# Layer A's dilated attention: the first group in time order with two key chunks, its softmax joined to the others' by shares

## What is computed

```python
DILATED_PAIRS = ((128, 1), (512, 4), (2048, 16))     # window, dilation of each group
def mixer_a(hn, w_in, w_out, q_gain, k_gain, t5_bias):
    proj = hn @ w_in                                  # 3 groups x (q, k, v), and a gate
    ...
    for g, (window, dilation) in enumerate(DILATED_PAIRS):
        q = rms_norm(qkv[:, :, g, 0], q_gain[g])
        k = rms_norm(qkv[:, :, g, 1], k_gain[g])
        v = qkv[:, :, g, 2]
        reach = (window // 2) // dilation             # keys at 0, +-d, ..., +-reach*d
        o, lse = dilated_group_attention(q, k, v, t5_bias[...], dilation, reach)
        outs.append(o)
        lses.append(lse)
    alpha = jax.nn.softmax(jnp.stack(lses), axis=0)   # groups merged by their denominators
    y = jnp.sum(alpha[..., None] * jnp.stack(outs), axis=0)
    y = y.reshape(b, s, BRANCH_WIDTH).astype(hn.dtype) * jax.nn.silu(gate)
    return y @ w_out
```

## Time and profile before

| | value |
|---|---|
| median of three runs | 1672.38 us |
| the profiled execution: its own time | 1674.71 us |
| its span (first to last instruction) | 1672.9 us |
| mean granted TensorE clock | 0.978 |
| busy share PE, DVE, ACT, POOL | 94%, 45%, 46%, 47% |
| layer A in it | about 26 to 712 us |
| mean of one low part on POOL (L919, 128x512; L899, 128x1024) | 1293 ns; 2477 ns |

### The profile page before, as it was taken

The page is one execution under the profiler, slowest core; times in us unless marked ns, Lnnn a source line. Parts: engine busy times, 40 slices in busy tenths (PEclk is TensorE's granted clock), DMA queues, the critical chain, the costliest instruction groups (busy, mean ns, idle before and its releaser), DMA issues. The chain is left out here.

```text
span 1672.9 us, 29914 instructions
## 1 busy us (share of the span) xinstructions
...
## 2 busy tenths in 40 slices
...
GB/s 180 120 59 94 71 96 80 76 101 67 101 70 104 74 90 1 63 149 139 143 154 134 76 51 88 115 70 63 26 28 3 4 3 28 88 89 101 90 92 57
DMA packets 247185, 135.44 MB, mean 81 GB/s; under 512 B 24390, under 2 KB 241518, under 8 KB 246999
## 3 DMA queue, kind: packets, MB, share of 16 engines
...
...
## 5 line engine op out<-in xcount | busy, mean ns | idle before, releaser
L919 POOL TENSOR_TENSOR a_sq_low<-a_sq,a_sq_high 128x512 fp32r<-128x512 f32 x48 | 62.1, 1293 | 278.4 <-ACT a_sq_high L766 278.4
L318 PE MATMUL a_proj<-h_low,w_high 128*128 128x512 f32 x472 | 190.0, 402 | 1.6 <-POOL h_low L938 0.8
L899 POOL TENSOR_TENSOR w_low<-a_w_raw,w_high 128x1024 fp32r<-128x1024 f32 x64 | 158.5, 2477 | 65.8 <-ACT w_high L733 65.8
L320 PE MATMUL a_proj<-h_high,w_high 128*128 128x512 f32 x472 | 185.7, 393 | 0.0
L319 PE MATMUL a_proj<-h_high,w_low 128*128 128x512 f32 x472 | 184.8, 392 | 0.0
L899 POOL TENSOR_TENSOR w_low<-b_w_raw,w_high 128x1024 fp32r<-128x1024 f32 x40 | 100.4, 2512 | 97.1 <-ACT w_high L733 97.1
L318 PE MATMUL b_proj<-h_low,w_high 128*128 128x512 f32 x288 | 116.5, 405 | 1.4 <-POOL h_low L938 0.8
L320 PE MATMUL b_proj<-h_high,w_high 128*128 128x512 f32 x288 | 113.5, 394 | 0.0
L319 PE MATMUL b_proj<-h_high,w_low 128*128 128x512 f32 x288 | 113.2, 393 | 0.0
L819 ACT ACTIVATE a_pt<-a_turned 128x512 f32<-128x512 f32 x64 | 37.8, 591 | 155.8 <-PE a_turned L612 155.8
L318 PEld LDWEIGHTS a_proj<-h_low,w_high 128*128 128x128 f32 x472 | 88.8, 188 | 23.4 <-DVE a_qk L969 3.2
...
## 6 DMA issues: line engine op xcount, KB each, us to landing
a_w_raw<-in_a_w_in_dram SPq DMA_DIRECT2D x78, 512.0 KB, 3.7
b_w_raw<-in_b_w_in_dram SPq DMA_DIRECT2D x30, 512.0 KB, 4.1
b_ada_w<-in_ada_w_dram ACTq DMA_DIRECT2D x24, 512.0 KB, 3.7
f_wt<-in_w_in_dram SPq DMA_DIRECT2D x19, 512.0 KB, 3.8
...
sparse_w_raw<-in_w_in_dram SPq DMA_DIRECT2D x17, 512.0 KB, 3.8
a_w_raw<-in_a_w_out_dram SPq DMA_DIRECT2D x8, 512.0 KB, 3.6
b_w_raw<-in_b_w_out_dram SPq DMA_DIRECT2D x8, 512.0 KB, 3.6
```

Source lines behind the costliest of these rows:

```text
L318: nc.tensor.matmul(out, lh, rl, start=first, stop=False)
L320: return nc.tensor.matmul(out, lh, rh, start=False, stop=last)
L899: nc.gpsimd.tensor_tensor(low(slot_of(b)), raw[:, n % RAW, :, :], high(slot_of(b)), ALU.subtract).then_inc(s_wl, 1)
L919: nc.gpsimd.tensor_tensor(sql[:, :], sq[:, u % 2, :], sqh[:, :], ALU.subtract).then_inc(s_sql, 1)
```

## The change

`attention_layer(nc, T, I, a)` is replaced by a function of its own, `dilated_attention` (layer B keeps `attention_layer`). Group 0's queries are now grouped in order of time: tile t holds 128 consecutive tokens, and its keys are 256 consecutive tokens, in two chunks of 128. Groups 1 and 2 stay by residue. So a step has 4 key chunks a head instead of 6. Since a token of group 0 and the same token of groups 1 and 2 lie in different tiles and rows, each part has its own peak and total; when all four tiles have them, they are copied crosswise between partitions (`swap`), and a chain on DVE and ACT (`shares`, `weights`) makes each part's share, with which the probabilities are then scaled. v of group 0 is projected as an eighth ring unit (V0, features by tokens) and turned at the end of the period (VT); the v units are 256 wide. The output of a pair is gathered in a bank of its own over the four tiles. The gate's reciprocal on DVE is two instructions on ACT. The bias of a head comes in 17 DMAs from the SP queue, 34 for a pair, ahead of the next weight block. In the last pair (`LAST`) three output units begin early (`e` for units 0 and 1, `f` for unit 2).

```diff
+    NQK, GATE, V0, VT = 6, 6, 7, 12
+    UNITS, NR, VB, RAW = 13, 8, 2, 2
+    EARLY, ROWS = 3, 4
+    STEPS = PAIRS * ROWS
+    VW = 3 * P
+    WIN, BIAS = 256, 6 * P
+    V_AFTER = (2, 4)
+    ROLL = ((16, 0, 112), (0, 112, 128))
+    HEAD_BANKS = [0, 1, 2, 3, 4, 5, 6, 0, 1, 2, 3, 1, 0]
+    IN_SCORES, IN_TURNED, IN_O = 11, 6, 7
+    SQUARES_AT = [(2, 5), (3, 3), (4, 2), (5, 1), (6, 1), (6, 6)]
...
+    PERIOD = [("S", 0), ("u", 0), ("S", 1), ("u", 1), ("S", 2), ("u", 2), ("S", 3), ("u", 3), ("u", 4),
+              ("T", 0), ("u", 5), ("A", 0), ("T", 1), ("u", 6), ("A", 1), ("T", 2), ("u", 7), ("A", 2), ("T", 3), ("u", 8),
+              ("u", 9), ("A", 3), ("u", 10), ("u", 11), ("u", 12)]
+    LAST = [("S", 0), ("e", 0), ("S", 1), ("e", 1), ("S", 2), ("e", 2), ("S", 3), ("e", 3), ("e", 4), ("e", 5),
+            ("e", 6), ("T", 0), ("f", 0), ("f", 1), ("A", 0), ("T", 1), ("f", 2), ("f", 3), ("A", 1), ("T", 2), ("f", 4), ("f", 5),
+            ("A", 2), ("T", 3), ("f", 6), ("A", 3), ("e", 7), ("f", 7)]
+    plan = lambda p: PERIOD if p < PAIRS - 1 else LAST
...
+            def load_bias(head):
+                h = head % 2
+                if head >= 2:
+                    sp.wait_ge(s_l2, 8 * (head // 2 - 1) + 7 + h)
+                at = lambda row, x: head * A_ROWS * REL + row * REL + x
+                for n, (x0, j0, j1) in enumerate(((80, 16, 32), (112, 0, 32), (80, 0, 32), (112, 0, 16))):
+                    for c in range(4):
+                        dst = bias[32 * c:32 * c + 32, h, n * P:(n + 1) * P].rearrange("p (c j) -> p c j", c=4)[:, :, j0:j1]
+                        sp.dma_start(dst, bass.AP(tensor=I["scr_a"].tensor, offset=at(c, x0 + j0),
+                                                  ap=[[1, 32], [REL, 4], [1, j1 - j0]])).then_inc(s_bias[h], 16)
+                sp.dma_start(bias[:, h, 4 * P:], bass.AP(tensor=I["scr_a"].tensor, offset=at(7, 0),
+                                                         ap=[[1, P], [REL, 2], [1, P]])).then_inc(s_bias[h], 16)
...
+            sp.wait_ge(T.s_scr, 128)
+            sp.wait_ge(s_neg, 4)
+            for head in range(2):
+                load_bias(head)
+            bias_after = {place["ring", NR * p + 6 + RING]: p for p in range(1, PAIRS)}
+            for n in range(RAW, len(order)):
+                sp.wait_ge(s_wl, n - RAW + 1)
+                load(n)
+                if n in bias_after:
+                    for h in range(2):
+                        load_bias(2 * bias_after[n] + h)
...
+                elif u == VT:
+                    pe.wait_ge(s_pf, UNITS * p + V0 + 1)
+                    for c in range(4):
+                        mm = nc.tensor.transpose(out[:, c * P:(c + 1) * P], vfm[:, c * P:(c + 1) * P], T.ident)
+                else:
+                    c = u - NR
+                    if c == 0:
+                        pe.wait_ge(s_wl, place["v", p, VB - 1] + 1)
...
+            def scores(p, t):
+                if t == 0:
+                    pe.wait_ge(s_pf, UNITS * p + NQK if p else IN_SCORES)
+                if p or t:
+                    pe.wait_ge(s_l2, 2 * (4 * p + t))
+                for n in range(4):
+                    for h in range(2):
+                        hp = slice(h * HD, (h + 1) * HD)
+                        g, k0 = (0, 32 * ((t + n) % 4)) if n < 2 else (n - 1, t * P)
+                        keys = qk[hp, p % 2, 2 * g + 1, :]
+                        keys = runs(keys, k0, k0 + 32) if g == 0 else keys[:, k0:k0 + P]
+                        out = ps_s[:, h, n * P:(n + 1) * P]
+                        mm = nc.tensor.matmul(out.rearrange("p (c j) -> p c j", c=4) if g == 0 else out,
+                                              qk[hp, p % 2, 2 * g, t * P:(t + 1) * P], keys, start=True, stop=True)
+                        if n == 3:
+                            mm.then_inc(s_S, 1)
...
+            def apply_v(p, t):
+                if t == 0:
+                    pe.wait_ge(s_pf, UNITS * (p + 1) if p else UNITS)
+                    if p:
+                        pe.wait_ge(s_y, p)
+                pe.wait_ge(s_pa, 4 * p + t + 1)
+                pe.wait_ge(s_pbk, 4 * p + t + 1)
+                for c, (tile, g) in enumerate(((t, 0), ((t + 1) % 4, 0), (t, 1), (t, 2))):
+                    for h in range(2):
+                        o = ps_o[h * HD:(h + 1) * HD, :]
+                        into = by_time(o)[:, :, 3 - t, :] if g == 0 else o[:, (3 - t) * P:(4 - t) * P]
+                        moving = pt[:, h, c, :].rearrange("p (c j) -> p c j", c=4) if g == 0 else pt[:, h, c, :]
+                        mm = nc.tensor.matmul(into, vt[:, p % 2, tile, g * P + h * HD:g * P + (h + 1) * HD], moving,
+                                              start=(t == 0 and c == 0), stop=(t == 3 and c == 3), skip_group_check=True)
+                mm.then_inc(s_O, 1)
...
+            def exps(p, t):
+                for h in range(2):
+                    act.wait_ge(s_l2, 2 * (4 * p + t) + h + 1)
+                    for part in range(2):
+                        e = probs[:, t, h, part * WIN:(part + 1) * WIN]
+                        nc.scalar.activation(e, e, ACT.Exp, scale=-1.0, bias=stat[:, own, part, t, h, 0:1],
+                                             accum_out=stat[:, own, part, t, h, 1:2]).then_inc(s_exp, 1)
+            def weights(p):
+                act.wait_ge(s_chain, CHAIN * p + 3)
+                nc.scalar.activation(diff[:, :, :], diff[:, :, :], ACT.Exp).then_inc(s_ew, 1)
...
+            def soft_peak(p, t):
+                n = 4 * p + t
+                if p:
+                    dve.wait_ge(s_Ta, n - 3)
+                    dve.wait_ge(s_Tb, n - 3)
+                for h in range(2):
+                    dve.wait_ge(s_bias[h], 16 * 17 * (p + 1))
+                    dve.wait_ge(s_S, 2 * n + h + 1)
+                    tiles = bias[:, h, 0:4 * P].rearrange("p (n j) -> p n j", n=4)
+                    near = tiles[:, 0:2, :] if t == 0 else tiles[:, 2:4, :] if t == 3 else tiles[:, 2:0:-1, :]
+                    two = lambda a: a.rearrange("p (n j) -> p n j", n=2)
+                    nc.vector.tensor_tensor_reduce(two(probs[:, t, h, 0:WIN]), two(ps_s[:, h, 0:WIN]), near, -1.0, HUGE,
+                                                   ALU.add, ALU.min, stat[:, own, 0, t, h, 0:1])
+                    nc.vector.tensor_tensor_reduce(probs[:, t, h, WIN:], ps_s[:, h, WIN:], bias[:, h, 4 * P:], -1.0, HUGE,
+                                                   ALU.add, ALU.min, stat[:, own, 1, t, h, 0:1]).then_inc(s_l2, 1)
+            def swap(p, t):
+                dve.wait_ge(s_exp, 4 * (4 * p + t + 1))
+                for b in range(4):
+                    rows, into = slice(32 * b, 32 * b + 32), slice(32 * (3 - t), 32 * (3 - t) + 32)
+                    nc.vector.tensor_copy(stat[into, other, 1, 3 - b, :, :], stat[rows, own, 0, t, :, :]).then_inc(s_swap, 1)
+                    nc.vector.tensor_copy(stat[into, other, 0, 3 - b, :, :], stat[rows, own, 1, t, :, :]).then_inc(s_swap, 1)
+            def shares(p):
+                done = lambda i: dve.wait_ge(s_chain, CHAIN * p + i)
+                flat = lambda who, s: stat[:, who, :, :, :, s].rearrange("p q t h -> p (q t h)")
+                dve.wait_ge(s_swap, 32 * (p + 1))
+                nc.vector.tensor_tensor(lead[:, :], flat(own, 0), flat(other, 0), ALU.min).then_inc(s_chain, 1)
+                done(1)
+                for who in (own, other):
+                    nc.vector.tensor_tensor(diff[:, who, :], lead[:, :], flat(who, 0), ALU.subtract).then_inc(s_chain, 1)
+                dve.wait_ge(s_ew, p + 1)
+                nc.vector.tensor_tensor(lead[:, :], diff[:, other, :], flat(other, 1), ALU.mult).then_inc(s_chain, 1)
+                nc.vector.tensor_tensor(flat(other, 0), diff[:, own, :], flat(own, 1), ALU.mult).then_inc(s_chain, 1)
+                done(5)
+                nc.vector.tensor_tensor(lead[:, :], lead[:, :], flat(other, 0), ALU.add).then_inc(s_chain, 1)
+                done(6)
+                nc.vector.reciprocal(lead[:, :], lead[:, :]).then_inc(s_chain, 1)
+                done(7)
+                nc.vector.tensor_tensor(share[:, :, :, :].rearrange("p q t h -> p (q t h)"), diff[:, own, :], lead[:, :],
+                                        ALU.mult).then_inc(s_chain, 1)
+                done(8)
+            def normal(p, t):
+                for h in range(2):
+                    for part in range(2):
+                        e = probs[:, t, h, part * WIN:(part + 1) * WIN]
+                        nc.vector.tensor_scalar(e, e, share[:, part, t, h:h + 1], None, ALU.mult).then_inc(s_pn, 1)
...
+            for u in range(UNITS):
+                take(0, u)
+            for p in range(PAIRS):
+                for kind, i in plan(p):
+                    if kind == "S":
+                        soft_peak(p, i)
+                        swap(p, i)
+                        if i == 3:
+                            shares(p)
```

(15 more changed lines are left out.)

418 lines of the change are left out of this document (388 added, 30 removed).

## The result

The changed kernel takes 1737.39 us (median of 4 runs, 1735.57 to 1738.91) against 1672.20 for the kernel before: a ratio of 1.0388, 95% interval 1.0370 to 1.0406. It is slower by 65 us, outside the range of the prediction. Its profiled execution took 1738.8, its span is 1737.0.

The account below looks back on a forecast made before the run. PE's own work was taken to bound the seven full periods. Start +3.7, periods -9.7 and last pair -12.0 gave -18.0: from 1674.7 to 1656.7, or 1654 us since the profiled run lay 2.3 over the median; range 1640 to 1708.

Parts of the forecast that it names:

- PE's work: In a full period of layer A, PE's own work without waits falls by 4.7 us to 72.2.
- The first wait: In each period PE waits 1.9 us (0.5 to 3.5) for unit 4's bank, behind the joined softmax on DVE.
- The second wait: 34 bias DMAs on SP's weight queue delay a load ACT needs; PE waits 0.2 us before the last application of v.
- q: Time SP needs to start one bias piece: taken as 0.50 us, bounds 0.37 to 0.64.
- Rival A: Bias pieces starve the weights: at 0.64 us each, PE waits 5.0 us per period; 1709 us in all, chance 0.34.
- The clock behind both waits: Loss at half clock after PE's waits in a full period: 0.85 us charged, half of an earlier 1.6.
- The start: Start of layer A: PE waits 7.7 us behind the 34 pieces; first scores come 3.7 us later (0 to 9).
- The last pair: From its first scores to the last product's end: 64.4 us, 12.0 less (8 to 14).

Follow-up runs that it names:

- the four edits: Changed kernel with y's rounding ahead of the exponentials, bias DMAs one weight block later, unit 2's take ahead of the shares, reductions for copies: 1653.1 us.
- five edits: The four edits plus the first two heads' 34 bias pieces issued after the load of the ninth block: 1643.9 us, ratio 0.9826.
- all six edits: The kernel with five edits, but in the last pair ACT rounds two blocks of y ahead of each tile: 1639.4 us, ratio 0.9804.

## Why the prediction was wrong

**PE's work: right.** I had 72.2 us for a period without waits; with the four edits it is 72.76, and with five PE is busy for 72.66 of 73 at clock 1.00. The product of 256 columns, which I had to read off a line at 0.121, is 0.117 (304.47 to 305.64 are ten of them). The Trainium skill (TensorE: Matmul & The Clock Gate, Back-to-back issue gap), which gives the formula that I used for an isolated product, has 0.109; the measurement decides. A block of scores costs 1.09 from its start to the next (123.86 to 124.95 in the kernel after), 1.07 forecast. In the period behind 240.21 of the kernel with five edits the four v units take 11.4 for 12.0, the four steps 11.8 for 11.4, the eight units with their sums 48.7 for 47.9, and 0.3 is a wait for a unit's squares. The gain that the change was to bring is there in the main: 3.7 us a period on the mean of seven, 4.1 against the 76.88 of one full step, where I had 4.7.

**The first wait: the step that failed is "Eight small copies at the pace of the small ones (three in 0.28) take 0.7".** The frame was right: exponentials start 3.1 us after unit 2 (3.2 forecast), end at 5.1 (5.2), PE wants unit 4 at 7.3 (7.2), the take costs 0.75 (0.75). But the copies take 3.1 (129.12 to 132.25) and not 0.7, and 2.1 of the 2.4 missing are one copy held by POOL. The shares cost 1.8 for 1.5 and the scalings 1.1 for 0.8. So the wait was 4.66 and not 1.9, outside my own 0.5 to 3.5, which varied only how long an operation works. POOL's low parts of 2.48 stood in my own sum for the second wait, and I never laid one beside DVE's copies. (My terms add up to 8.95 and not to 9.1; that slip is small.)

**The second wait: q was right, the landing was not.** I took 0.50 for a piece; 32 of 34 cost 0.478. The step that failed is "then the next weight load, 3.7 to land": with the median of all loads the block is there 28.6 us after unit 4 ended. It was there at 31.0: the pieces began at 7.8 (7.9 forecast) and took 17.8 for 17.0, with the last at 1.89, and the load behind them landed after 5.4 and not 3.7. PE arrives after 30.2 (30.0 forecast), so a sum that left 1.4 us of slack before the two operations on ACT met a chain that was 2.4 longer, and PE waits 2.33 on the mean for 0.2. Rival A named this mechanism and the right place, but tied it to q of 0.64 and began it at 0.55; it came at 0.478. Of its price for the clock, 2.2 us a period, 1.4 came (the experiment with the bias DMAs later). That A's period of 82.2 is nearly the measured 82.12 is luck: A had 1.9 and 5.0 us for the two waits, and they are 4.66 and 2.33.

**The clock behind both waits.** I charged 0.85 us, half of what the earlier trace rows showed behind a wait of 2.08, as if two waits cost no more than one. Of the period of 82.12, 72.75 are work and 7.0 waits; what is left, 2.4, is the half clock behind them, nearly three times my figure.

**The start: right.** +3.7 forecast, +3.8 measured, with 8.6 us of waiting for 7.7. Part of that is luck, since here too the load behind the 34 pieces (16.3 us, 17 forecast) was there after 5.5 us and not 3.7, while from unit 4's first product to the first scores it took 39.1 us for 40.1.

**The last pair: the step that failed is "192 output products 44.5", taken as work that fills the waits for the tiles.** I gave 3 us to the tiles and let the output products fill the rest, without asking who makes their input. Each needs y's high part from ACT and the low part from POOL, and ACT has it in the program behind the exponentials of the same tile, whose scores PE only just did. So the filler arrived after the work that it was to cover, 22 us of waiting in four places, with the 1.2 GHz level behind each: +19.0 instead of -12.0. With y two blocks ahead of each tile the pair takes 68.8, 7.7 less than before and still 4.4 over my 64.4.

The time lies above rival A's range too (1680 to 1712). Of the miss of 83.4 us (1737.4 against 1654), 49.1 lie in the seven periods (82.12 for 75.1), 31.1 in the last pair, 0.1 at the start; 2.0 are where the first product comes, and the rest is how the profiled runs stand to the medians. The version with all six edits at 1639.4 shows that the estimate of PE's work was sound, and that the change's loss lay in the order on ACT, DVE and SP and in the choice of a copy for `swap`.
